# Products of zeros on TensorE around the transposes of norms and in the attention's last steps

## The chip, the cores and the metric

One core of one Trainium2 chip runs the whole program. The metric is the device time of one execution in microseconds (us); the median of the timed executions stands for a kernel.

## What is computed

A sequence of 256 tokens with 1024 features goes through one block of a first model and two layers of a second, all in float32:

```python
# first model, one block
h = rmsnorm(x, norm_mix);  proj = h @ w_in
x = x + concat([hgrn2(...), rglru(...), gla(...)]) @ w_out
h = rmsnorm(x, norm_ffn)
x = x + (gelu(causal_dwconv(h @ ffn_w_gate)) * (h @ ffn_w_val)) @ ffn_w_down
x = rmsnorm(x, norm_final)
# second model, two layers
x = layer_norm(alpha * x + 0.5 * swiglu(x, w_gu[0], w_down[0]))
mix = token_mixers(x)        # window, latent (MLA), axial and differential attention, then @ w_out
x = layer_norm(alpha * x + mix)
x = layer_norm(alpha * x + 0.5 * swiglu(x, w_gu[1], w_down[1]))
```

The hidden width of the first feed-forward block is 2688 (21 tiles of 128), of the four others 2816 (22 tiles).

## The kernel before

**Precision.** Every large product is made of three with operands rounded to a shorter float (`F32R`): high by high, high by low and low by high (`mm3`, L782 to L785; `gate_up` joins two of them, L849 and L852). ScalarE rounds a weight tile (`weights_high`, L1316; `down_weights_high`, L1323), VectorE subtracts to get the rest (L1665, L1670). TensorE is the engine that has most to do.

**Order.** Each engine runs one program written out by hand, and they meet through semaphores. TensorE takes its instructions strictly in the order of `tensor_program`: a wait holds everything behind it. There are eight PSUM banks of 128 x 512 float32.

**Norm and transpose.** A norm is worked out on VectorE token by token, in two halves of 128 tokens (m = 0, 1). `turn(src, event, m)` (L787 to L794) then transposes the normed half on TensorE, eight 128 x 128 blocks (L793), the first four when `normed_v` says that columns 0 to 511 are there. ScalarE copies the bank, rounded (`turned_high`, L1328), VectorE subtracts (`turned_low`, L1680), and only then may the products with the normed half begin (`wait_h`, which waits for `h_low`).

**Feed-forward blocks.** `ffn(f, i, src)` (L894): f = 0 is that of the first model and turns both halves before its first product. For f = 1 to 4 the first two tiles are made per half (`gate_up_tokens`): half 0 is turned, both tiles are made for it, half 1 is turned, both tiles are made for that. The other tiles follow with all 256 tokens (`gate_up`), each with the `down` products of the tile before. With f = 1 and 3 the norm ahead follows another feed-forward block, with f = 2 and 4 it follows the attention's output product.

**Attention.** `first_projections(l)` (L1062) turns half 0, makes a chunk of the input projection for it, turns half 1, and goes on. `mixers(l)` then works through 20 units of attention (four window, four axial, eight differential, four MLA: units 0 to 19), in steps s = 0 to 20 (L1259). In step s TensorE makes, in this order: for even s the logits of units s+2 and s+3 (`logits`, L1190); the weighted sum of values of unit s-1 (`weighted`, L1221), which waits for ScalarE's copy of the transposed probabilities (L1596); while there are any, other projections; and the transposes of unit s's probabilities (`probabilities`, L1201). Steps 9 to 12 also transpose MLA's queries and keys into bank 5 (`latent_turn`, L1146), from where VectorE copies them out (L2100, signal `qk_copied`; the last is `qk_copied[l, "mla", 1, 2]`, in step 12). The exponentials are ScalarE's (L1585), the maxima VectorE's (L2057). In steps 17, 18 and 19 parts of the output product follow the probabilities (`out_part`).

`zeros` is a tile of 128 x 512 in bf16, all zero, which GpSimd clears at the very start; it is used by one product in `outputs` (L984).

Of the kernel before, what the change touches and what calls it, by code (L numbers as in the profile page):

```python
# [14 lines left out]
P = 128  # L15
# [153 lines left out]
def program(nc, A, C, out):  # L169
    ctx = ExitStack()  # L170
    with ctx:
        def sb(name, shape, dt=F32):
            return ctx.enter_context(nc.sbuf_tensor(name, shape, dt))

        bank = [ctx.enter_context(nc.psum_tensor(f"bank{i}", [P, HALF], F32)) for i in range(8)]
        signals = []

        def signal(name):
            signals.append(Signal(ctx.enter_context(nc.semaphore(name))))
            return signals[-1]  # L180
# [57 lines left out]
        qk_turned, qk_copied = signal("qk_transposed"), signal("qk_copied")  # L238
# [33 lines left out]
        zeros = sb("zeros", [P, HALF], BF16)  # L272
# [148 lines left out]
        def high_of(c):  # L421
            return (hi_out2 if third_place(c) else hi_out3) if outside_ring(c) else hi_gu[c % 2]

        def low_of(c):
            return (lo_out2 if third_place(c) else lo_out3) if outside_ring(c) else lo_gu[c % 2]
# [9 lines left out]
        def cols_view(t_, c):  # L435
            return t_[:, :].rearrange("p (k n) -> p k n", k=KD)[:, :, 0:width_of(c)]

        def pair_view(t_, c):
            return t_[:, :].rearrange("p (w k n) -> p w k n", w=2, k=KD)
# [40 lines left out]
        def tile_no(f, j):  # L480
            return FFN_FIRST[f] + j
# [5 lines left out]
        def wait_low(eng, c):  # L487
            s = wt_low_p if c in low_by_pool else wt_low_v
            eng.wait_ge(s.sem, s[c])
# [35 lines left out]
        def turn_bank(event, m, q):  # L525

            if event in (1, 2) or (isinstance(event, int) and event % 3 != 0):
                f = {1: 0, 2: 1}.get(event, 2 * ((event - 3) // 3) + (2 if event % 3 == 1 else 3))
                g1 = (FFN_FIRST[f] + 1) % 2
                return bank[(4 + g1, 6 + g1)[q]] if m == 0 else bank[q]  # L530
            if not isinstance(event, int):
                return bank[(6, 4)[q] + m]
            return bank[4 + 2 * m + q]
# [246 lines left out]
        def tensor_program(pe):  # L780

            def mm3(o, lhs, rhs, start, stop, **kw):  # L782
                pe.matmul(o, lhs[0], rhs[0], start=start, stop=False, **kw)  # L783
                pe.matmul(o, lhs[0], rhs[1], start=False, stop=False, **kw)  # L784
                return pe.matmul(o, lhs[1], rhs[0], start=False, stop=stop, **kw)  # L785

            def turn(src, event, m):  # L787

                for q in range(2):
                    if isinstance(event, int):  # L790
                        pe.wait_ge(normed_v.sem, normed_v[event, m, q])
                    for k in range(4 * q, 4 * q + 4):
                        t = pe.transpose(turn_bank(event, m, q)[:, (k % 4) * P:(k % 4 + 1) * P], src[:, m, k * P:(k + 1) * P], ident[:, :])  # L793
                    t.then_inc(h_turned.sem, h_turned.one((event, m, q)))  # L794

            def wait_h(event, m, k):
                if k % 4 == 0:
                    pe.wait_ge(h_low.sem, h_low[event, m, k // 4])
# [25 lines left out]
            def token_half(c, m, o, event=None):  # L824
                hv, lv = cols_view(high_of(c), c), cols_view(low_of(c), c)
                ms_ = slice(m * P, (m + 1) * P)
                wait_low(pe, c)
                for k in range(KD):
                    if event is not None:
                        wait_h(event, m, k)  # L830
                    i = mm3(o, (xTh[:, k, ms_], xTl[:, k, ms_]), (hv[:, k, :], lv[:, k, :]), k == 0, k == KD - 1)
                i.then_inc(tok_done.sem, tok_done.one((c, m)))
# [22 lines left out]
            def turn_products(g):  # L855

                t = g % 2
                pe.wait_ge(prod_done.sem, prod_done[g])
                for m in range(M):
                    i = pe.transpose(bank[4 + t][:, S + m * P:S + (m + 1) * P], act32[:, t, m * P:(m + 1) * P], ident[:, :])  # L860
                i.then_inc(act_turned.sem, act_turned.one(g))

            def gate_up_tokens(f, j, m, event=None, turned=None):

                g, c = tile_no(f, j), CHUNK_NO["ffn", f, j]
                o = bank[(4, 6)[m] + g % 2][:, 0:S].rearrange("p (w n) -> p w n", w=2)
                hv, lv = pair_view(high_of(c), c), pair_view(low_of(c), c)
                ts = slice(m * P, (m + 1) * P)
                wait_low(pe, c)
                for k in range(KD):  # L870
                    if event is not None:
                        wait_h(event, m, k)
                    if turned is not None and k == KD // 2:
                        turn_products(turned)
                    i = mm3(o, (xTh[:, k, ts], xTl[:, k, ts]), (hv[:, :, k, :], lv[:, :, k, :]), k == 0, k == KD - 1)
                done = tok_gate_up if m == 0 else up_done
                i.then_inc(done.sem, done.one(g))
# [16 lines left out]
            def ffn(f, i, src):  # L894
                tail = range(FFN_TILES[f] - TAIL, FFN_TILES[f])
                turn(src, i, 0)
                if f == 0:
                    turn(src, i, 1)
                else:

                    gate_up_tokens(f, 0, 0, i)
                    gate_up_tokens(f, 1, 0)
                    turn(src, i, 1)
                    gate_up_tokens(f, 0, 1, i)
                    gate_up_tokens(f, 1, 1, turned=tile_no(f, 0))
                    down(f, 0, 0)
                    turn_products(tile_no(f, 1))
                    down(f, 0, 1)
                for j in range(BY_TOKENS if f else 0, FFN_TILES[f]):
                    gate_up(f, j, i if j == 0 else None)  # L910
                    if 0 < j <= tail[0]:
                        for m in range(M):
                            down(f, j - 1, m)
                for m in range(M):
                    for j in tail:
                        down(f, j, m)
# [146 lines left out]
            def first_projections(l):  # L1063

                i = 3 + 3 * l
                c = CHUNK_NO["in2", l, 0]
                turn(x, i, 0)
                token_half(c, 0, bank[0][:, 0:WCOLS], i)
                turn(x, i, 1)

                pe.wait_ge(x_added.sem, x_added[i, 1, 0])
                token_half(c + 1, 0, bank[2][:, 0:width_of(c + 1)])
                token_half(c, 1, bank[1][:, 0:WCOLS], i)
                token_half(c + 1, 1, bank[3][:, 0:width_of(c + 1)])

            def mixers(l):
# [182 lines left out]
                for s in range(units + 1):  # L1259
                    if s + 2 < units and s % 2 == 0:  # L1260
                        logits(s + 2)
                    if s >= 1:
                        weighted(s - 1)
                    if s < len(BESIDE):
                        half(*BESIDE[s])
                    if s < units:
                        probabilities(s)
                    if s in (0, 1):
                        axial_turn(s)
                    if s == 2:  # L1270
                        latent_sums()
                    if 3 <= s <= 6:
                        up_projection((s - 3) // 2, (s - 3) % 2)
                    if 9 <= s <= 12:
                        latent_turn((s - 9) // 2, 2 * ((s - 9) % 2))
                    if s in (10, 11):
                        turn_mix(s - 10, 0)
                    if s == units - 3:

                        pe.wait_ge(exp_ok.sem, exp_ok[l, units - 3])  # L1280
                        out_part(1, 0, 0)
                        out_part(1, 1, 0)
                    if s == units - 2:
                        pe.wait_ge(exp_ok.sem, exp_ok[l, units - 2])
                        out_part(0, 0, 0)
                        out_part(0, 1, 0)
                    if s == units - 1:
                        pe.wait_ge(exp_ok.sem, exp_ok[l, units - 1])
                        out_part(0, 2, 0)
                        out_part(0, 3, 0)  # L1290
# [949 lines left out]
```

## Time and profile before

| | |
|---|---|
| median of 3 timed runs | 1430.88 us (1430.53 to 1436.68) |
| device time of the profiled execution | 1435.12 us |
| its span, first to last instruction | 1433.5 us |
| TensorE matmul busy | 1351.0 us, 94% of the span |
| VectorE busy | 917.1 us, 64% |
| ScalarE busy | 725.6 us, 51% |
| mean granted TensorE clock | 0.968 of full speed |

All times within the execution count from the span's start. "Busy" of TensorE counts the modelled ends of pipelined matmuls, so one of 128 x 512 is shown as 393 ns long while the next one starts 230 ns after it; the distance of starts is what an instruction costs. The granted clock is 1.0 at 2.4 GHz and 0.5 at 1.2 GHz; no other value occurs in this trace.

### The profile page before, as it was taken

Reading aid. Unit: us, or ns where it says so; the run is one execution under the profiler, and the core shown is the slowest. Engines: PE = TensorE matmul, PEld = TensorE weight load, DVE = VectorE, ACT = ScalarE, POOL = GpSimd, SP = SyncE. Lnnn points to the kernel's source line nnn. Section 1 sums busy time; section 2 is a strip of 40 time slices with the busy share of each in tenths; the row PEclk is TensorE's granted clock in tenths of the full one; section 3 lists DMA queues with packets and bytes.
Section 4 is the critical chain, followed back from the end, with each engine's and each line's share of the span. In section 5 each row is a group of like instructions: output and inputs, shape, how many; then the busy total and the mean of one; then the engine's idle time right before and its main releaser. Section 6 shows DMA issues by size and latency. Waiting matters only on the chain.

```text
span 1433.5 us, 20478 instructions
## 1 busy us (share of the span) xinstructions
PE 1351.0 (94%) x8221; PEld 1193.1 (83%) x8222; DVE 917.1 (64%) x1342; ACT 725.6 (51%) x1142; POOL 93.7 (7%) x137
## 2 busy tenths in 40 slices
PE   6888899998899999999899999999999999899997
PEld 6777888886788888888888888888888888888886
DVE  4787776777656658555666567656667464666556
ACT  5566455554455553564354554555553653354452
POOL 1233000000000000510000000000001400000000
PEclk9997999999999999998999999999999997999999
DMA  7333476665575664432476665666654332375661
GB/s 231 94 113 103 123 214 208 206 185 172 152 219 177 183 188 113 142 118 63 120 235 182 198 204 151 181 203 202 182 162 128 97 118 64 113 235 177 197 200 44
DMA packets 301191, 229.17 MB, mean 160 GB/s; under 512 B 13083, under 2 KB 283818, under 8 KB 301098
## 3 DMA queue, kind: packets, MB, share of 16 engines
q1 hardware_dynamic: 301082, 227.88, 52.8%
q8 instruction: 65, 1.06, 0.3%
q14 instruction: 28, 0.23, 0.0%
q10 hardware_dynamic: 16, 0.00, 0.0%
HBM read 226.80 MB, written 1.05 MB: 159 GB/s over the span
## 4 chain that ended last, share of the span: by engine, by line
PE 70%; DVE 15%; ACT 9%; DMA 3%; issue 2%; POOL 1%; SPq 0%; DVEq 0%; ACTq 0%
PE bank L849 20%; PE bank L783 11%; PE bank L852 10%; PE bank L784 10%; PE bank L785 10%; DVE lo_gu L1665 5%; ACT hi_gu L1316 4%; PE bank L1221 3%; DMA st_dn<-in_ffn_w_down 2%; PE bank L1190 2%; DVE lo_dn L1670 2%; PE bank L1201 1%; DVE conv L1830 1%; DVE stats L1692 1%; DVE n L1715 1%
## 5 line engine op out<-in xcount | busy, mean ns | idle before, releaser
L849 PE MATMUL bank<-xT,hi_gu 128*128 128x512 f32 x1616 | 404.8, 393 | 4.9 <-DVE lo_gu L1665 4.3
L1665 DVE TENSOR_TENSOR lo_gu<-st_gu,hi_gu 128x2048 fp32r<-128x2048 f32 (+2 forms) x146 | 323.4, 2218 | 111.9 <-ACT hi_gu L1316 111.8
L849 PEld LDWEIGHTS bank<-xT,hi_gu 128*128 128x128 f32 x1616 | 297.0, 189 | 64.4 <-DVE lo_gu L1665 6.4
L1316 ACT ACTIVATE hi_gu<-st_gu 128x2048 fp32r<-128x2048 f32 (+3 forms) x147 | 270.2, 1843 | 0.5 <-DMA st_gu<-in_ffn_w_gu 0.3
L852 PEld LDWEIGHTS bank<-xT,lo_gu 128*128 128x128 f32 x1616 | 220.8, 191 | 15.9
L852 PE MATMUL bank<-xT,lo_gu 128*128 128x256 f32 x1616 | 225.5, 282 | 0.0
L783 PE MATMUL bank<-hi_dn,actTh 128*128 128x512 f32 x436 | 172.4, 395 | 9.2 <-DVE actTl L1842 4.7
L784 PE MATMUL bank<-lo_dn,actTh 128*128 128x512 f32 x436 | 170.8, 392 | 0.0
L785 PE MATMUL bank<-hi_dn,actTl 128*128 128x512 f32 x436 | 169.7, 389 | 0.0
L1833 DVE TENSOR_TENSOR act<-act,bank 128x256 f32<-128x256 f32 x101 | 42.6, 421 | 174.2 <-ACT act L1413 174.2
L1323 ACT ACTIVATE hi_dn<-st_dn 128x1024 fp32r<-128x1024 f32 x109 | 114.6, 1056 | 67.9 <-DMA st_dn<-in_ffn_w_down 67.9
L1670 DVE TENSOR_TENSOR lo_dn<-st_dn,hi_dn 128x1024 fp32r<-128x1024 f32 x109 | 132.7, 1221 | 17.3 <-ACT hi_dn L1323 16.8
L783 PE MATMUL bank<-hi_gu,xT 128*128 128x256 f32 (+1 forms) x416 | 126.2, 303 | 10.7 <-DVE xT L1680 9.4
L784 PE MATMUL bank<-lo_gu,xT 128*128 128x256 f32 (+1 forms) x416 | 123.1, 296 | 0.0
L785 PE MATMUL bank<-hi_gu,xT 128*128 128x256 f32 (+1 forms) x416 | 122.9, 295 | 0.0
L783 PEld LDWEIGHTS bank<-hi_dn,actTh 128*128 128x128 f32 x436 | 82.2, 188 | 25.8 <-DVE actTl L1842 6.3
L783 PEld LDWEIGHTS bank<-hi_gu,xT 128*128 128x128 f32 x416 | 85.9, 206 | 14.2 <-issue 9.8
L785 PEld LDWEIGHTS bank<-hi_dn,actTl 128*128 128x128 f32 x436 | 81.9, 188 | 17.9
L784 PEld LDWEIGHTS bank<-lo_dn,actTh 128*128 128x128 f32 x436 | 82.2, 189 | 13.3
L784 PEld LDWEIGHTS bank<-lo_gu,xT 128*128 128x128 f32 x416 | 85.8, 206 | 0.0
L785 PEld LDWEIGHTS bank<-hi_gu,xT 128*128 128x128 f32 x416 | 85.5, 206 | 0.0
L1403 ACT ACTIVATE nonlin<-bank 128x256 f32<-128x256 f32 x101 | 38.3, 379 | 92.7 <-PE bank L852 92.6
(270 smaller groups left out, 1823.7 us busy)
## 6 DMA issues: line engine op xcount, KB each, us to landing
st_gu<-in_ffn_w_gu SPq DMA_DIRECT2D x176, 512.0 KB, 5.2
st_dn<-in_ffn_w_down SPq DMA_DIRECT2D x109, 512.0 KB, 6.6
st_gu<-in_w_in SPq DMA_DIRECT2D x23, 1024.0 KB, 5.4
st_gu<-in_w_out SPq DMA_DIRECT2D x12, 1024.0 KB, 5.1
st_gu<-in_ffn_w_gate SPq DMA_DIRECT2D x21, 512.0 KB, 4.2
st_gu<-in_ffn_w_val SPq DMA_DIRECT2D x21, 512.0 KB, 5.5
st_gu<-in_w_in SPq DMA_DIRECT2D x10, 512.0 KB, 4.1
gb<-in_ln_g SPq DMA_DIRECT2D x6, 512.0 KB, 7.3
```

The source lines that it names most:

```text
L783: pe.matmul(o, lhs[0], rhs[0], start=start, stop=False, **kw)
L784: pe.matmul(o, lhs[0], rhs[1], start=False, stop=False, **kw)
L785: return pe.matmul(o, lhs[1], rhs[0], start=False, stop=stop, **kw)
L849: pe.matmul(b[:, :], hv[:, w, k, :], xT[:, k, :, :].rearrange("p a b -> p (a b)"), start=k == 0, stop=k == KD - 1, skip_group_check=True)
L852: i = pe.matmul(b[:, 0:S], lv[:, w, k, :], xTh[:, k, :], start=False, stop=k == KD - 1, skip_group_check=True)
L1221: t = pe.matmul(bank[4][:, z * HD:(z + 1) * HD], ptb[:, u % 2, (2 * z + kt) * P:(2 * z + kt + 1) * P], vb[:, kt, v0 + vh * HD:v0 + (vh + 1 ...
L1316: i = act.activation(high, staged, ACT.Copy)
L1323: act.activation(hi_dn[g % RING][:, :], st_dn[g % 2][:, :], ACT.Copy).then_inc(dn_high.sem, dn_high.one(g))
L1403: act.activation(nonlin[:, t, :], gate[:, S:2 * S], ACT.Copy).then_inc(gate_side.sem, gate_side.one(g))
L1665: i = dve.tensor_tensor(low, staged, high.bitcast(F32), ALU.subtract)
L1670: dve.tensor_tensor(lo_dn[g % RING][:, :], st_dn[g % 2][:, :], hi_dn[g % RING][:, :].bitcast(F32), ALU.subtract).then_inc(dn_low.sem, dn_l ...
L1833: dve.tensor_tensor(act32[:, t, :], act32[:, t, :], up[:, 0:S], ALU.add).then_inc(own_v.sem, own_v.one())
```

## The change

A helper `fill(b, count)` issues `count` products of the tile of zeros into a bank that nobody reads at that time. Each is 128 x 128 by 128 x 512 in bf16. No other instruction, wait, buffer or transfer is changed, but for one added wait: in step 13 of each attention, ahead of the first fill into bank 5, TensorE waits for VectorE's copy of the last MLA keys out of that bank.

```diff
+            def fill(b, count):
+                for _ in range(count):
+                    pe.matmul(bank[b][:, :], zeros[:, 0:P], zeros[:, :], start=True, stop=True, skip_group_check=True)
...
             def ffn(f, i, src):
                 tail = range(FFN_TILES[f] - TAIL, FFN_TILES[f])
                 turn(src, i, 0)
+                idle = 6 + tile_no(f, 0) % 2
+                fill(idle, 3)
                 if f == 0:
                     turn(src, i, 1)
+                    fill(idle, 4)
                 else:
                     gate_up_tokens(f, 0, 0, i)
                     gate_up_tokens(f, 1, 0)
+                    fill(idle, 4)
                     turn(src, i, 1)
+                    fill(idle, 3)
                     gate_up_tokens(f, 0, 1, i)
...
                 turn(x, i, 0)
+                fill(7, 3)
                 token_half(c, 0, bank[0][:, 0:WCOLS], i)
+                fill(7, 6)
                 turn(x, i, 1)
...
                 for s in range(units + 1):
                     if s + 2 < units and s % 2 == 0:
                         logits(s + 2)
+                    if s >= 13:
+                        if s == 13:
+                            pe.wait_ge(qk_copied.sem, qk_copied[l, "mla", 1, 2])
+                        fill(5, 2)
                     if s >= 1:
                         weighted(s - 1)
```

Products of zeros added: 7 in block f = 0, 10 in each of f = 1 to 4, 9 in each of the two `first_projections`, and 16 in the steps 13 to 20 of each attention: 97 in all.

## Rows read from the trace of the kernel before

**Rows 1.** The page: the chain that ended last, share of the span by engine.

```profile
PE 70%; DVE 15%; ACT 9%; DMA 3%; issue 2%; POOL 1%; SPq 0%; DVEq 0%; ACTq 0%
```

**Rows 2.** Windows: stretch, us, busy of PE, PEld, DVE, ACT, POOL (count), PEclk, DMA.

```profile
170.00:176.80 6.80, 5.93 (x18) 4.79 (x19) 6.64 (x9) 4.37 (x5) 0.00 (x0) 0.50 0.25 74
...
1183.70:1204.20 20.50, 19.13 (x74) 16.95 (x74) 9.21 (x23) 7.47 (x22) 0.00 (x0) 0.50 0.00 1
1241.70:1248.60 6.90, 6.06 (x29) 6.03 (x29) 4.39 (x7) 4.53 (x8) 0.00 (x0) 0.51 0.40 123
```

**Rows 3.** The same view: just ahead of one fall, and a stretch without one.

```profile
702.40:705.80 3.40, 1.75 (x12) 1.31 (x13) 2.69 (x4) 1.84 (x3) 0.00 (x0) 1.00 0.19 46
...
634.20:637.60 3.40, 2.53 (x24) 2.29 (x23) 2.54 (x5) 2.76 (x10) 0.00 (x0) 1.00 0.00 0
```

**Rows 4.** Timeline of TensorE, f = 2, 4, 1: start, us, line, tiles [idle before, releaser].

```profile
703.20 1.32 PE L793 MATMUL bank<-ident,x 128*128 128x128 f32 x8 [1.97 <-DVE x L1722]
714.15 0.50 PE L783 MATMUL bank<-hi_dn,actTh 128*128 128x512 f32 x1 [1.10 <-DVE actTl L1812]
...
1240.44 1.32 PE L793 MATMUL bank<-ident,x 128*128 128x128 f32 x8 [1.97 <-DVE x L1722]
1252.54 0.50 PE L783 MATMUL bank<-hi_dn,actTh 128*128 128x512 f32 x1 [1.10 <-DVE actTl L1812]
...
370.01 0.36 PE L783 MATMUL bank<-hi_gu,xT 128*128 128x256 f32 x1 [1.07 <-DVE xT L1680]
377.32 0.50 PE L783 MATMUL bank<-hi_dn,actTh 128*128 128x512 f32 x1 [1.10 <-DVE actTl L1812]
```

**Rows 5.** The same view, the first two turns of f = 1 and f = 3.

```profile
362.09 0.36 PE L783 MATMUL bank<-hi_gu,xT 128*128 128x256 f32 x1 [0.84 <-DVE xT L1680]
367.91 1.04 PE L793 MATMUL bank<-ident,x 128*128 128x128 f32 x8
...
890.22 0.55 PE L783 MATMUL bank<-hi_gu,xT 128*128 128x256 f32 x1 [0.84 <-DVE xT L1680]
897.54 1.03 PE L793 MATMUL bank<-ident,x 128*128 128x128 f32 x8
```

**Rows 6.** The same view, second turn ahead of each attention, and a later wait in it.

```profile
557.04 1.32 PE L793 MATMUL bank<-ident,x 128*128 128x128 f32 x8 [1.85 <-DVE x L1722]
591.54 1.10 PE L1221 MATMUL bank<-proj,big 128*128 128x64 f32 x8 [0.45 <-ACT big L1596]
...
1086.67 1.32 PE L793 MATMUL bank<-ident,x 128*128 128x128 f32 x8 [1.84 <-DVE x L1722]
1124.33 1.10 PE L1221 MATMUL bank<-proj,big 128*128 128x64 f32 x8 [0.45 <-ACT big L1596]
```

**Rows 7.** Timeline, layer 1: VectorE's copy of step 12, TensorE in steps 14 to 17.

```profile
1180.50 0.69 DVE L2100 TENSOR_SCALAR big<-bank 96x512 f32<-96x512 f32 x1
...
1183.47 3.49 PE L1190 MATMUL bank<-big 96*128 96x256 f32 x8 [1.21 <-ACT big L1585]
...
1192.72 3.62 PE L1190 MATMUL bank<-big 96*128 96x256 f32 x8
1196.13 1.81 PE L1221 MATMUL bank<-proj,big 128*128 128x64 f32 x8
...
1201.95 0.56 PE L783 MATMUL bank<-hi_gu,xT 128*128 128x256 f32 x1
```

**Rows 8.** Timeline of layer 0's steps 14 to 17, TensorE.

```profile
650.68 3.19 PE L1190 MATMUL bank<-big 96*128 96x256 f32 x8 [1.21 <-ACT big L1585]
...
662.28 1.00 PE L1221 MATMUL bank<-proj,big 128*128 128x64 f32 x8
664.42 1.10 PE L1221 MATMUL bank<-n,big 128*128 128x64 f32 x8 [0.69 <-ACT big L1596]
...
665.72 0.36 PE L783 MATMUL bank<-hi_gu,xT 128*128 128x256 f32 x1
```

**Rows 9.** Chain of waits: start, us, eight products of 128 x 512, rounded operands, full speed.

```profile
392.37 1.84 PE bank L849 x8
```

## The prediction, as it was put on record

> **What bounds the kernel now.** I read the page first: TensorE carries 70% of the chain that ended last [rows 1] and is busy for 94% of the span. VectorE and ScalarE come in where TensorE waits for a norm, for a copy of transposed probabilities, or for weights in block f = 0. So two things can shorten this kernel: less waiting of TensorE, or more work per microsecond while it runs. The second view is the granted clock by windows. Its mean is 0.968, and there are only two levels, 2.4 and 1.2 GHz. Cutting the trace where the level changes gives seven stretches at 1.2 GHz in places that the change touches: 170.0 to 176.8 (f = 0), 651.3 to 661.5 (layer 0's last steps), 705.9 to 709.3 (f = 2), 890.2 to 893.6 (f = 3), 1088.2 to 1095.0 (ahead of layer 1's attention), 1183.8 to 1204.2 (layer 1's last steps) and 1241.8 to 1248.6 (f = 4). The first, the longest and the last stand in [rows 2]. They add up to 58 us, nearly all with TensorE busy. Four more lie before 143 us, which the change leaves alone.
>
> The third view is what TensorE did just before a fall. Ahead of that at 705.9 it was busy for 1.75 of 3.40 us and half of that were transposes; in a stretch at 634.2 it was busy for 2.53 of 3.40 us with small products, and the clock stayed up [rows 3]. So falls follow stretches in which TensorE waits once or twice for one or two microseconds and does little between. The same places in the other layer or block are not always hit: f = 1 and the projections ahead of layer 0's attention kept 2.4 GHz. That gives a clean twin for most places, and I price the falls by these twins, not by the length of a stretch.
>
> **What the falls cost.** All are differences of start times between a slowed place and its twin at full speed.
> - f = 2: from the second turn to the first `down` product 714.15 - 703.20 = 10.95 us; f = 1 takes 377.32 - 367.91 = 9.41 [rows 4, 5]. Lost: 1.5 us.
> - f = 4: 1252.54 - 1240.44 = 12.10 us [rows 4]. Lost: 2.6 us (its turn begins as f = 2's does; 0.1 taken off for that turn's own wait between its quads, in both).
> - f = 3: from the first product to the second turn 897.54 - 890.22 = 7.32 us against 367.91 - 362.09 = 5.82 in f = 1 [rows 5]. Lost: 1.5 us.
> - Ahead of layer 1's attention: 1124.33 - 1086.67 = 37.66 us against 591.54 - 557.04 = 34.50 in layer 0 [rows 6]. Lost: 3.2 us. Nothing in between gives it back; this is measured past every copy on the other engines.
> - Last steps. At full speed one pair of steps (logits, then twice a weighted sum and a set of transposes) is 665.72 - 662.28 = 3.44 us for all but the logits [rows 8], with one wait of 0.69 inside, plus the logits, which take 1196.13 - 1192.72 = 3.41 at 1.2 GHz [rows 7], so an estimated 1.7 at 2.4. A pair: 5.15 us; the steps 14 to 17 are two pairs, 10.3 us. Layer 0 took 665.72 - 650.68 = 15.04 (lost: 4.7), layer 1 took 1201.95 - 1183.47 = 18.48 (lost: 8.2), and it stayed slow for another 2.3 us of dense output products, half of which is lost: 9.3 in all. I take 9.0, since a little of that ending shows as overlap.
> - f = 0: no twin. TensorE is busy for 5.93 us at 1.2 GHz [rows 2], so 3.0 us at most. But the chain through this block runs over VectorE, ScalarE and the `down` weights' transfers, not over TensorE; what moves this chain is only the turn, whose eight transposes take 1.32 us at full speed [rows 4], so about 0.7 us more at half. I take 0.7, the lower end, because the chain is what ends later waits there.
>
> Sum if every one of these falls is avoided: 0.7 + 4.7 + 1.5 + 1.5 + 3.2 + 9.0 + 2.6 = 23.2 us.
>
> **What the products of zeros cost.** No row times a bf16 product of zeros. The nearest is the rounded 128 x 512 product at full speed, eight in 1.84 us, 0.23 us each [rows 9]; bounds are 0.2 and, if it runs at 1.2 GHz, 0.46. I take 0.23. Each group is set against the wait it stands in.
> - Three after a turn, 0.7 us: the wait there is 0.84 or 1.07 us [rows 4, 5], ended by VectorE's subtraction, which does not start later for it. Hidden; at 1.2 GHz they would stick out by 0.5.
> - Four ahead of the second turn, 0.9 us: in f = 2 and 4 the wait is 1.97 us [rows 4]; hidden. In f = 1 and 3 there is no wait before the second turn [rows 5]: the norm was done in time. There the four stand bare, and ScalarE's and VectorE's work on the turned half starts as much later. 0.9 us each, 1.8 in all.
> - f = 0: three in a wait of over 2 us, four in the one after the second turn; hidden, the latter barely.
> - Ahead of the attentions: three in a wait like the 0.84 one, six (1.4 us) in the wait of 1.85 [rows 6]. Hidden.
> - Steps 13 to 20, two each. Step 13 adds a wait for VectorE's copy, which ends at 1181.19 [rows 7]; unit 12's weighted sum started at 1180.72, so it starts about a microsecond later, and behind it unit 13's transposes. But TensorE then waited 1.21 us for an exponential before the next logits [rows 7], and that exponential does not hang on the delayed steps. Cost: 0, up to 0.5. Steps 15 and 17 have the wait of 0.69 ahead of the weighted sum [rows 8]: two products are 0.46, hidden. Steps 14 and 16 put them behind the logits, which already hide the copy, and steps 18 to 20 behind dense output products: no wait, so bare. Five steps x 2 x 0.23 = 2.3 us per layer, 4.6 in all.
>
> Sum: 1.8 + 4.6 = 6.4 us. Queues of the other engines and all transfers keep their order; they are released earlier or at most 0.9 us later.
>
> **The sum.** Against the profiled execution's own 1435.12 us: 1435.1 - 23.2 + 6.4 = 1418.3. Two kinds of sparse stretch get no fill: the differential units at about 632 and 1165 us, and waits of block f = 0 near 338 and 351 us. In this trace no fall followed them, but their like did elsewhere. I add 1.7 us for one short fall: 1420. The profiled execution lies 4.2 us above the median of 1430.88; I don't shift for that, because which places are hit seems to vary by execution (three runs span 6 us), and with the fills in place there is less left to vary.
>
> **A rule that speaks against.** The falls here come after single waits of 1.0 to 2.6 us. The Trainium skill ("TensorE: Matmul & The Clock Gate", "Why this matters for your kernels") asks only that TensorE not idle for one gap longer than any of these. By that rule these waits cause no fall and filling them helps nothing; the trace disagrees, with seven falls in just these places. Its Part 1 also says that operands of all zeros don't trip another limiter, of current; whether zeros count as activity for this clock no row here shows.
>
> **The rivals.**
> 1. *The zeros don't hold the clock, and cost.* The falls stay, and the bare products are paid, those at 1.2 GHz doubly: 6.4 us, plus 0.5 to 1 us for steps 14 and 16 of both layers, plus 0.5 each in places where a covered group sticks out of its wait in a slowed turn: about 8. Place: the steps 14 to 20, where TensorE is the bound. 1435.1 + 8 = 1443, or 1439 against the median. It decides as soon as fewer than 6.4 us of falls are avoided. For it: no row shows zeros raising the clock. Against: even light products at 634.2 held it [rows 3].
> 2. *Norms are cured, the last steps are not.* Two products are only 0.46 us, and the wait ahead of step 14's logits keeps most of its length. Then 9.5 us are won around norms and 6.4 to 8 us paid: 1433.
> 3. *The gain is handed on.* The falls go, but ScalarE's exponentials or VectorE's weight splits become the bound in the last steps and in f = 0, and half of the steps' 13.7 us is lost again: 1427. Against: in layer 0 from 662.28 on the steps ran at full speed with only the 0.69 waits [rows 8].
>
> **Chances.** Forecast (1415 to 1424) 0.64; rival 1 0.10; rival 2 0.10; rival 3 and partial cures 0.16. The range 1413 to 1431 takes in the forecast with its bounds (f = 0 giving 3.0 instead of 0.7; fills at 0.2; two or three leftover falls) and rival 3; it leaves out 1 and 2. A measurement can tell about 0.5%, so faster means below 1423.7 and slower above 1438.0 us: faster 0.70, same 0.22, slower 0.08.
>
> **What would show it.** In the profile after, the seven stretches should stand at 1.0, with the distances above at 9.4 (f = 2 and 4, second turn to `down`), 34.5 (second turn to step 0's wait) and about 11.2 us for steps 14 to 17 (10.3 and two bare pairs). A turn at f = 1 and 3 0.9 us later than its twin shows the bare fours. If the level still falls behind filled waits, zeros don't count or are too few; if it stays up and the time doesn't move, look for a new wait on ScalarE at L1585 or L1596. The forecast is wrong if a fill costs well over 0.23 us, or if new falls appear in the unfilled stretches.

## The result and the profile after

The changed kernel takes 1419.38 us (median of 14 runs, 1417.01 to 1423.47) against 1430.7 us for the kernel before, measured beside it (14 runs, 1421.86 to 1440.82). The ratio is 0.9916, with a 95% interval from 0.989 to 0.994: faster by 0.8%. The forecast was 1420 us, and its range 1413 to 1431. What the medians don't say is how much steadier the time became: 19 us between the fastest and the slowest run before, 6.5 us after.

| | before | after |
|---|---|---|
| device time of the profiled execution | 1435.12 us | 1417.01 us |
| its span | 1433.5 us | 1415.4 us |
| TensorE matmul busy | 1351.0 us | 1350.2 us |
| mean granted TensorE clock | 0.968 | 0.986 |

TensorE is busy for the same time with 97 products more, because the other products have become shorter. The page of the changed kernel, chain by engine, where [rows 1] stood before:

```profile
PE 70%; DVE 16%; ACT 9%; issue 2%; DMA 2%; POOL 1%; SPq 0%; DVEq 0%; ACTq 0%
```

The shares of the chain have hardly moved. Nothing was taken off it by a shorter dependency; the same chain is walked faster.

Windows of the changed kernel (stretch, us, busy of PE, PEld, DVE, ACT, POOL with counts, PEclk, DMA share, GB/s): the steps 14 to 17 of both layers, the second turn of f = 2, and the two stretches around the second turn of f = 0.

```profile
649.80:661.10 11.30, 10.79 (x72) 8.88 (x73) 8.13 (x20) 5.78 (x20) 0.00 (x0) 1.00 0.01 2
1174.90:1186.20 11.30, 10.79 (x72) 8.88 (x73) 8.21 (x20) 5.78 (x20) 0.00 (x0) 1.00 0.01 2
701.00:704.40 3.40, 3.21 (x25) 2.61 (x23) 2.90 (x4) 3.32 (x5) 0.00 (x0) 1.00 0.03 5
...
166.50:169.90 3.40, 1.50 (x12) 0.87 (x10) 2.89 (x8) 1.29 (x3) 0.00 (x0) 1.00 0.00 0
170.00:173.30 3.30, 3.30 (x12) 2.05 (x11) 3.25 (x6) 2.47 (x4) 0.00 (x0) 0.50 0.00 0
```

Layer 1's steps, which had 0.50 for 20.5 us [rows 2], are at 1.00. Of the seven slowed stretches six are gone. The one at the start of f = 0 is left, half as long as before, and in this execution a fall of 3.4 us at 337 us is new. Apart from these two only the falls before 143 us remain, which the change doesn't touch, and one from 1412.4 us to the end, where TensorE has no work left (the kernel before had it too, from 1429.5 us).

The timeline of the changed kernel's TensorE at the places of [rows 4 to 8] (start, us, line, tiles, idle before and its releaser; the line of every added product is L799):

```profile
891.25 1.04 PE L799 MATMUL bank<-zeros 128*128 128x512 bf16 x4
892.12 1.04 PE L793 MATMUL bank<-ident,x 128*128 128x128 f32 x8
892.99 0.81 PE L799 MATMUL bank<-zeros 128*128 128x512 bf16 x3
894.22 0.36 PE L783 MATMUL bank<-hi_gu,xT 128*128 128x256 f32 x1 [0.42 <-DVE xT L1699]
...
697.79 1.04 PE L799 MATMUL bank<-zeros 128*128 128x512 bf16 x4
699.92 1.32 PE L793 MATMUL bank<-ident,x 128*128 128x128 f32 x8 [1.09 <-DVE x L1741]
709.37 0.50 PE L783 MATMUL bank<-hi_dn,actTh 128*128 128x512 f32 x1 [1.10 <-DVE actTl L1831]
...
1225.02 1.32 PE L793 MATMUL bank<-ident,x 128*128 128x128 f32 x8 [1.09 <-DVE x L1741]
1234.46 0.50 PE L783 MATMUL bank<-hi_dn,actTh 128*128 128x512 f32 x1 [1.10 <-DVE actTl L1831]
...
1081.22 1.32 PE L793 MATMUL bank<-ident,x 128*128 128x128 f32 x8 [0.53 <-DVE x L1741]
1115.72 1.10 PE L1235 MATMUL bank<-proj,big 128*128 128x64 f32 x8 [0.45 <-ACT big L1615]
...
1172.63 0.61 PE L799 MATMUL bank<-zeros 128*128 128x512 bf16 x2 [0.78 <-DVE big L2119]
1174.86 1.96 PE L1204 MATMUL bank<-big 96*128 96x256 f32 x8 [0.34 <-ACT big L1604]
1176.66 0.60 PE L799 MATMUL bank<-zeros 128*128 128x512 bf16 x2
1178.38 0.59 PE L799 MATMUL bank<-zeros 128*128 128x512 bf16 x2
1179.22 1.11 PE L1235 MATMUL bank<-proj,big 128*128 128x64 f32 x8 [0.26 <-ACT big L1615]
1182.34 0.60 PE L799 MATMUL bank<-zeros 128*128 128x512 bf16 x2
1182.78 1.00 PE L1235 MATMUL bank<-proj,big 128*128 128x64 f32 x8
1186.21 0.36 PE L783 MATMUL bank<-hi_gu,xT 128*128 128x256 f32 x1
```

Two kinds of added product can be told apart here. The four at 697.79 end before the wait for the norm does: the idle time ahead of the turn went from 1.97 [rows 4] to 1.09 us, and the turn didn't move. The four at 891.25 have no idle time behind them: the turn starts 0.87 us later, four times 0.218 us, and everything after it too. In the steps, the pair at 1178.38 only shortens a wait (0.69 to 0.26), the pair at 1182.34 is followed at once by the weighted sum, which starts 0.44 us after it.

**Where the time went**, as differences of the two profiles between starts of the same instruction (before minus after; gains positive):

| stretch | forecast | measured |
|---|---|---|
| up to f = 0's second turn (untouched) | 0 | 0.6 |
| f = 0, to its end | 0.7 | 1.2 |
| f = 1 (bare four) | -0.9 | -0.9 |
| ahead of layer 0's attention and its steps to 13 | 0 | 0 |
| layer 0, steps 14 to 17 | 4.7 - 0.9 | 3.7 |
| layer 0, steps 18 to 20, to f = 2's second turn | -1.4 | -1.3 |
| f = 2's second turn to first `down` | 1.5 | 1.5 |
| f = 3, net of its bare four | 0.6 | 0.6 |
| ahead of layer 1's attention | 3.2 | 3.2 |
| layer 1, steps 14 to 20, to f = 4's second turn | 9.0 - 2.3 | 6.8 |
| f = 4's second turn to first `down` | 2.6 | 2.7 |
| sum | 16.8 | 18.1 |

These are two single executions. The one before took 4.4 us more than the median of its kernel, the one after is the fastest of its 14; so they differ by 18.1 us and the medians by 11.3.

The new fall at 337 us cost nothing. TensorE at that place, first in the kernel before, then in the changed kernel:

```profile
338.74 2.12 PE L849 MATMUL bank<-xT,hi_gu 128*128 128x512 f32 x8 [2.48 <-DVE lo_gu L1665]
351.95 0.50 PE L783 MATMUL bank<-hi_dn,actTh 128*128 128x512 f32 x1 [2.90 <-DVE actTl L1842]
...
336.98 3.62 PE L854 MATMUL bank<-xT,hi_gu 128*128 128x512 f32 x8 [2.15 <-DVE lo_gu L1684]
350.19 0.51 PE L783 MATMUL bank<-hi_dn,actTh 128*128 128x512 f32 x1 [1.68 <-DVE actTl L1861]
```

Eight products took 3.62 instead of 2.12 us, but the changed kernel is 1.76 us ahead at the first pair of lines and 1.76 us ahead at the second: the wait at 350 us became shorter by what the fall took.

### The profile page after: what moved, and what is told of

Read it like the earlier page. It is cut to its first block, busy times and chain, and to the rows that moved or that the text cites. A ratio compares the mean times of both kernels' runs of the same rounds, so it can differ in the third digit from the quotient of the medians.

```text
span 1415.4 us, 20673 instructions
## 1 busy us (share of the span) xinstructions
PE 1350.2 (95%) x8319; PEld 1182.6 (84%) x8319; DVE 917.4 (65%) x1342; ACT 724.6 (51%) x1142; POOL 92.8 (7%) x137
## 4 chain that ended last, share of the span: by engine, by line
PE 70%; DVE 16%; ACT 9%; issue 2%; DMA 2%; POOL 1%; SPq 0%; DVEq 0%; ACTq 0%
PE bank L854 20%; PE bank L857 11%; PE bank L783 10%; PE bank L784 10%; PE bank L785 10%; DVE lo_gu L1684 5%; ACT hi_gu L1335 4%; PE bank L1235 2%; DVE lo_dn L1689 2%; PE bank L1204 2%; DMA st_dn<-in_ffn_w_down 2%; DVE conv L1849 1%; PE bank L1215 1%; DVE stats L1711 1%; DVE n L1734 1%
## 5 line engine op out<-in xcount | busy, mean ns | idle before, releaser
L783 PE MATMUL bank<-hi_gu,xT 128*128 128x256 f32 (+1 forms) x416 | 121.6, 292 | 4.2 <-DVE xT L1699 2.9
L784 PE MATMUL bank<-lo_gu,xT 128*128 128x256 f32 (+1 forms) x416 | 118.9, 286 | 0.0
L785 PE MATMUL bank<-hi_gu,xT 128*128 128x256 f32 (+1 forms) x416 | 118.6, 285 | 0.0
L783 PEld LDWEIGHTS bank<-hi_gu,xT 128*128 128x128 f32 x416 | 81.1, 195 | 10.3 <-issue 6.6
L1432 ACT ACTIVATE act<-bank 128x256 f32<-128x256 f32 x101 | 38.2, 378 | 88.9 <-PE bank L857 88.9
L783 PE MATMUL bank<-xT,hi_gu 128*128 128x256 f32 x248 | 73.4, 296 | 8.3 <-ACT proj L1502 4.5
```

Of the source, the lines that this page charges most:

```text
L1432: act.activation(act32[:, t, :], up[:, S:2 * S], ACT.Copy).then_inc(up_side.sem, up_side.one(g))
```

## The experiments

Each kernel was timed beside the kernel before on the same chip, in four sets of runs: one for `e1` to `e4`, one for `e5` to `e8`, one for `e9` to `e11`, one for `e12`. The medians of the kernel before in them were 1430.6, 1435.9, 1431.1 and 1430.2 us. `C` stands below for the changed kernel.

**Norms alone, steps alone.** `e1_norms` leaves out the products of the steps:

```diff
-                    if s >= 13:
-                        if s == 13:
-                            pe.wait_ge(qk_copied.sem, qk_copied[l, "mla", 1, 2])
-                        fill(5, 2)
```

> The products of zeros around the norms' transposes stay (65), those in steps 13 to 20 and their wait are gone (32 fewer). My theory (each group only hinders falls of the clock at its own place): no half-clock stretch at the starts of f = 1 to 4 and ahead of the attentions; the last steps of the attentions fall in some executions, up to 4.7 us in layer 0 and 9 us in layer 1, while 4.6 us of bare products are saved. So about 1421 us with a wide spread (1413 to 1428). Rival (the fills of the steps did most of the work): 1427 or more.

Measured: 1417.45 us median of 11 runs, 1415.24 to 1430.08. `e2_steps` leaves out every `fill` around a `turn`:

```diff
                 turn(src, i, 0)
-                idle = 6 + tile_no(f, 0) % 2
-                fill(idle, 3)
...
-                fill(7, 3)
                 token_half(c, 0, bank[0][:, 0:WCOLS], i)
-                fill(7, 6)
```

> Only the products of zeros in steps 13 to 20 stay (32); those around norms are gone. My theory: steps 14 to 17 keep 2.4 GHz in both layers, 11.5 us for both pairs; the starts of f = 2 and 4 and the second turn ahead of the attentions fall in most executions, of 9.5 us together about two thirds; 1.8 us of bare products in f = 1 and 3 saved: about 1424 us. Rival (norms alone matter, the steps' products only cost): 1435.

Measured: 1427.21 us median of 12 runs, 1419.07 to 1431.92. It lies 3 us above the 1424 that I expected and 8 below the rival's 1435. Windows of `e1_norms` (layer 0's last steps, then from f = 2's second turn, 704.11, on), and of `e2_steps` (f = 2's second turn, ahead of layer 1's attention, and layer 0's last steps):

```profile
652.20:662.20 10.00, 9.31 (x35) 8.11 (x34) 4.65 (x10) 3.51 (x14) 0.00 (x0) 0.50 0.00 1
704.10:711.00 6.90, 6.69 (x50) 5.86 (x51) 5.02 (x8) 4.99 (x8) 0.00 (x0) 1.00 0.24 75
```

```profile
706.30:713.00 6.70, 5.88 (x28) 5.80 (x28) 4.22 (x6) 4.55 (x8) 0.00 (x0) 0.50 0.37 112
1088.60:1098.70 10.10, 10.10 (x49) 9.96 (x48) 5.51 (x9) 1.19 (x2) 0.00 (x0) 0.50 0.39 104
650.00:661.00 11.00, 9.62 (x68) 8.04 (x69) 8.61 (x22) 6.35 (x17) 0.00 (x0) 1.00 0.00 1
```

Each group acts where it stands. Where the steps have none, layer 0's still ran for 10 us at 0.50; where the norms have none, both places after a second turn did, and the steps did not. The median of `e1_norms` is below `C`'s 1419.38, better than I expected: without the steps' 20 bare products 4.4 us are saved in every run, and the falls come back in some only. The slowest run, 1430.08 us, had a mean clock of 0.974, the fastest, 1415.24, one of 0.984; which places fell in the slowest can't be seen, since it has no trace. Against `e3_covered` below, which has twelve products in the steps but not the eight bare ones of f = 1 and 3 (1.7 us), the median, with these 1.7 us taken off, is only 2.3 us higher, the slowest run 13. So the steps' products save little in a typical execution and much in a bad one.

**Only the products that stand in a wait.** `e3_covered`:

```diff
-                    fill(idle, 4)
+                    if f % 2 == 0:
+                        fill(idle, 4)
...
-                        fill(5, 2)
+                        if s in (13, 15, 17):
+                            fill(5, 2)
```

> The changed kernel without the products that stand in no wait: the four ahead of the second turn in f = 1 and 3, and those of steps 14, 16, 18, 19 and 20. 69 products stay, all in waits. My theory: these 28 bare ones cost 28 x 0.22 = 6.2 us and hindered no fall, so 1413 us, with the clock at 1.0 in the same places. Rival (the bare ones in the steps keep the clock up, since the steps' waits are spread over all of them): falls come back in steps 14 to 17, 1418 us or more with a wider spread.

Measured: 1413.4 us median of 6 runs, 1411.16 to 1414.89; ratio to the kernel before 0.988 (0.985 to 0.992). Its windows over the last steps of layer 0 and the start of f = 2:

```profile
651.80:662.20 10.40, 9.89 (x67) 8.46 (x68) 8.01 (x20) 5.80 (x20) 0.00 (x0) 1.00 0.01 2
701.00:705.00 4.00, 3.80 (x30) 3.23 (x28) 3.69 (x4) 3.91 (x6) 0.00 (x0) 1.00 0.10 13
```

So 28 of the 97 products cost 6.0 us (1419.4 - 1413.4) and did nothing. The traces agree: from the first turn of f = 1 to the second of f = 4, `C` takes 1225.02 - 358.17 = 866.85 us and `e3_covered` 1221.80 - 361.09 = 860.71, which is 6.14 us less, 0.219 for each of the 28. The last steps' clock doesn't need them.

**Is it busy time, or any instruction?** `e4_thin` keeps the count and the places and cuts the length to 16 columns; `e6_half` cuts it to 256:

```diff
-                    pe.matmul(bank[b][:, :], zeros[:, 0:P], zeros[:, :], ...)
+                    pe.matmul(bank[b][:, 0:16], zeros[:, 0:P], zeros[:, 0:16], ...)    # e4_thin
+                    pe.matmul(bank[b][:, 0:S], zeros[:, 0:P], zeros[:, 0:S], ...)      # e6_half
```

> The same 97 products of zeros in the same places, each with 16 columns in place of 512: the same count, the same weight loads, hardly any busy time. If what holds the clock is how long TensorE is kept busy (my theory), the falls stay as in the kernel before: about 1431 us, plus at most 28 x 0.06 = 1.7 us for bare ones, with the wide spread of the kernel before. If it is enough that TensorE is given some instruction in a wait (rival), the falls go: about 1413 us.

Measured: 1429.19 us median of 12 runs, 1420.72 to 1438.04; ratio to the kernel before 0.999 (0.996 to 1.002). The line of the added products in its trace (duration in ns, least, median and most; first and last start), and its windows over layer 1's last steps and the start of f = 2:

```profile
L799 PE MATMUL bank<-zeros x97: 169/170/221, 168.8 to 1241.1; 128*128 128x16 bf16 x97
1182.40:1202.70 20.30, 19.01 (x81) 17.07 (x79) 8.85 (x22) 6.95 (x21) 0.00 (x0) 0.50 0.00 1
701.00:707.80 6.80, 6.30 (x32) 5.96 (x31) 4.48 (x7) 4.81 (x7) 0.00 (x0) 0.50 0.20 65
```

All 97 are there and the falls are too. It is not the instruction but how long it occupies the array.

> The same 97 products in the same places with 256 columns in place of 512: half the busy time. If it is the busy time that holds the clock, halving it makes part of the falls come back (mostly at the starts of f = 2 and 4 and at step 14, hardly ahead of the attentions, where nine products stand), while the bare ones cost 28 x 0.11 = 3 us less: about 1420 us with a wide spread, 1414 to 1428. If full length was more than needed: 1416 us with the narrow spread of the changed kernel.

Measured: 1416.96 us median of 9 runs, 1415.36 to 1420.15, with a spread as narrow as `C`'s. The expectation of falls coming back was mostly too gloomy: its trace has none at the starts of f = 1 to 4. One came where only two products stand, at 1173.6 us in the logits of layer 1's step 14, and was over at 1177.0, at that step's pair (1176.53); f = 0's, which full length doesn't cure either, is there too. The 2.4 us below `C` are most of what the bare ones cost less (28 x 0.11 = 3.1). Full length was more than the norms' waits needed.

**The price of a bare product.** `e5_price` adds a hundred where TensorE has no wait:

```diff
                 wait_low(pe, c)
+                if f in (1, 3) and 5 <= j < 10:
+                    for _ in range(10):
+                        pe.matmul(gate[:, :], zeros[:, 0:P], zeros[:, :], start=True, stop=True, skip_group_check=True)
```

> The changed kernel with 100 more products of zeros in dense stretches: ten each ahead of the gate products of tiles 5 to 9 of f = 1 and f = 3, where TensorE is the bound and has no wait, so each costs its full price. If a bare product costs 0.22 us, as the distances in the changed kernel's trace say, 1419.4 + 22 = 1441 us; if it costs 0.23 or more, 1442.5 or more; if VectorE's and ScalarE's work had slack to hide it, less.

Measured: 1442.44 us median of 12 runs, 1438.08 to 1444.59. Two of its tiles on the timeline:

```profile
426.73 2.33 PE L850 MATMUL bank<-zeros 128*128 128x512 bf16 x10
428.71 2.18 PE L857 MATMUL bank<-xT,hi_gu 128*128 128x512 f32 x8
431.68 2.00 PE L857 MATMUL bank<-xT,hi_gu 128*128 128x512 f32 x8
437.22 2.33 PE L850 MATMUL bank<-zeros 128*128 128x512 bf16 x10
```

A tile takes 437.22 - 426.73 = 10.49 us, against 8.31 without (400.68 - 392.37 in the chain of the kernel before): 0.218 us each, so 21.8 for a hundred. The medians say 23.1 (1442.44 - 1419.38), but the two kernels were timed in different sets of runs. Nothing hides them.

**Where the fall in the steps is fought.** `e8_no13` takes from `e3_covered` step 13's two products and the added wait; `e9_only13` takes those of steps 15 and 17:

```diff
-                    if s >= 13:
-                        if s == 13:
-                            pe.wait_ge(qk_copied.sem, qk_copied[l, "mla", 1, 2])
-                        if s in (13, 15, 17):
-                            fill(5, 2)
+                    if s in (15, 17):          # e8_no13
+                        fill(5, 2)
...
-                        if s in (13, 15, 17):
+                        if s == 13:            # e9_only13
                             fill(5, 2)
```

> The kernel with the covered products alone, without those of step 13 and the wait added there; steps 15 and 17 keep theirs. If the sparse stretch of steps 13 and 14 is what starts the fall (my theory), it is now as bare as in the kernel before: the fall comes in some executions, but steps 15 and 17 are busier than before, so it may end sooner: median 1415 us, highest above 1420. If the products of steps 15 and 17 carry the effect, or the fall has no fixed origin: 1413 us with the narrow spread.

Measured: 1412.53 us median of 6 runs, 1411.62 to 1413.56. The narrow spread is what the rival said, and no fall in the steps stands in its trace. Theory B of the next expectation was formed on this.

> The kernel with the covered products alone, without those of steps 15 and 17: of the last steps only step 13 has its two products and its wait. Theory A (they hinder the fall where it starts, between steps 13 and 14): about 1413 us with the narrow spread of the covered kernel. Theory B, after the kernel without those of step 13 stayed at 1412.5 us within 2 us, and the changed kernel's repeat e5 showed one fall at 647 us that ended after 3.4 us: the products of steps 15 and 17 don't stop the fall, they end it early. Then without them a fall here lasts as long as in the kernel before, 10 to 20 us in some executions: median 1414 to 1418 us, the highest above 1420.

Measured: 1413.9 us median of 6 runs, 1413.2 to 1415.66: theory B's long falls didn't come. One of its premises was a misreading as well: the fall at 647.3 us in the trace of `e5_price` is not one of the last steps. The added products delay that kernel, so that its step 13 begins with the pair at 660.64 us; the fall lies among the differential units, where no product of zeros stands, and ended without one. By `e8_no13` and `e9_only13` alone either group seems to be enough. The next kernels say more.

**More of it.** `e7_more` adds to `e3_covered`:

```diff
-                fill(idle, 3)
+                fill(idle, 7 if f == 0 else 3)
...
+                if f == 0 and j == 19:                       # gate_up
+                    pe.wait_ge(gate_summed.sem, gate_summed[g - 2])
+                    fill(4 + g % 2, 6)
                 wait_low(pe, c)
...
+                        if f == 0 and m == 0 and j == tail[-1]:
+                            fill(5, 7)
                         down(f, j, m)
...
+                if lev == 0:                                 # levels of the first model's scores
+                    pe.wait_ge(cleared_p.sem, cleared_p["zeros"])
+                if lev in (3, 6, 8):
+                    copied = t_copied_a if lev == 3 else tok_copied_a
+                    pe.wait_ge(copied.sem, copied[{3: 7, 6: 10, 8: 11}[lev], 0])
+                    fill(6, 6)
...
+            pe.wait_ge(selected.sem, selected[LEV_N - 1, 0, 0])
+            fill(0, 5)
             pe.wait_ge(selected.sem, selected[LEV_N - 1, 3])
...
+                    if s == 9:
+                        wait_projected(pe, l, 8, 0)
+                        fill(6, 3)
```

> The kernel with the covered products alone (1413.4 us), and more of them in waits that had none: ahead of levels 3, 6 and 8 of the first model's scores and of the last head outputs, seven instead of three between the two turns of f = 0, six and seven in the two waits at the end of f = 0, and three ahead of the weighted sum of step 9. In the trace of the covered kernel 20 us at half clock remain in those places before 145 us and at 352 us, of which some 15 us are within reach. My theory: most of them go and half their length is won, 1408 us. Rival (they collide with the copies that the added waits ask for, or VectorE and ScalarE bind there and nothing is won): 1413 to 1416 us.

Measured: 1410.72 us median of 6 runs, 1410.12 to 1412.56; ratio 0.986 (0.981 to 0.991). The fastest version of the study, but the gain over `e3_covered` is 2.7 us where I expected 5. Windows of its repeat (`e12_more_again`, below):

```profile
50.00:57.00 7.00, 3.67 (x17) 3.67 (x18) 3.96 (x4) 3.99 (x6) 2.60 (x1) 0.65 0.00 0
112.00:119.00 7.00, 6.59 (x64) 5.44 (x66) 6.63 (x10) 1.66 (x4) 0.73 (x1) 1.00 0.42 138
130.00:142.00 12.00, 9.13 (x65) 8.16 (x65) 8.23 (x15) 7.11 (x9) 5.83 (x3) 0.86 0.39 132
```

The kernel before and `e3_covered` went through the place at 112 us at half clock. That it is cured is not shown by this window: the trace of `C` has 1.00 there too, without a product, and fell at 81.2 us instead. But each of the eleven traces without these additions has a short fall somewhere between 80 and 121 us, and none of the three with them. The place at 50 us follows a wait of 4.5 us into which I found no bank to put a product; at 134.1 us a fall is left, and another follows at 147.7.

What was gained can be placed by the traces. Block f = 0, from its second turn to the first turn of f = 1, takes 187.7 to 187.8 us in the three traces with the additions, 189.6 in that of `e3_covered` and 188.3 to 190.0 in all with three products between its turns. What lies before it gained 0.1 us in `e7_more` and 1.4 in `e12_more_again`, against `e3_covered`.

`e10_best` is the same without step 13's products and wait:

> The kernel with more products in more waits, without those of step 13 and its wait. If each part does what it did alone (1410.7 us for more, 0.9 us less without step 13): 1410 us, between 1409 and 1412. If step 13's products are needed after all: a spread beyond 4 us.

Measured: 1414.36 us median of 6 runs, 1410.71 to 1416.19. Its profiled execution shows why. Timeline of TensorE from step 13 on, and one window:

```profile
647.27 0.61 PE L1229 MATMUL bank<-ident,big 128*128 128x128 f32 x4
649.08 3.71 PE L1218 MATMUL bank<-big 96*128 96x256 f32 x8 [1.21 <-ACT big L1618]
652.59 1.80 PE L1249 MATMUL bank<-proj,big 128*128 128x64 f32 x8
655.04 1.05 PE L799 MATMUL bank<-zeros 128*128 128x512 bf16 x2
655.93 1.10 PE L1249 MATMUL bank<-proj,big 128*128 128x64 f32 x8
657.32 1.89 PE L1218 MATMUL bank<-big 96*128 96x256 f32 x8
649.20:655.90 6.70, 6.70 (x22) 5.18 (x22) 4.50 (x8) 1.80 (x7) 0.00 (x0) 0.50 0.00 0
```

The wait of 1.21 us ahead of step 14's logits is whole again, the fall comes right after it, and it is over at the next pair of products, in step 15, after 6.7 us instead of 10 to 20. It cost 2.9 us: step 14's logits start 0.48 us later than in the trace of `e12_more_again` (649.08 against 648.60), the first turn of f = 2 starts 3.40 us later (689.90 against 686.50). The repeat of `e7_more` was to tell chance from cause:

> The kernel with more products in more waits, step 13's included, once more and on another start. If the products of step 13 are what keeps the fall away there (theory A), it stays within 3 us of spread around 1411 us, as in its first job, where the same kernel without them spread over 5.5 us. If that spread was chance, it is now as wide as that one, with a median near 1413 us.

Measured: 1410.93 us median of 6 runs, 1410.26 to 1412.21, at a ratio of 0.986 (0.982 to 0.991). Twelve runs with step 13's products now span 2.4 us, six without them 5.5 us, and four of these six are slower than all twelve. I read it so: step 13's two products hinder the fall, and those of step 15, when it has come, are followed by its end. Neither half is shown. For the first, `e8_no13` against `e3_covered` says the opposite (1.9 us of spread without them, 3.7 with them), and that its six runs just didn't meet the fall is my guess. For the second there are two falls, this one and that of `e6_half`; and in the kernel before layer 0's fall ended at 661.5 us, in the middle of the steps, with no product of zeros near.

Last, the changed kernel again, on the chip of `e9_only13` and `e10_best`:

> The changed kernel once more, on the chip of the two others. Against it the bare products' price is read without a change of chip: 1419.4 us within 1.5, so 6 us above the kernel with the covered ones alone, and its trace shows which falls are left in an execution with another start.

Measured: 1419.19 us median of 12 runs, 1416.51 to 1423.03; 5.3 us above `e9_only13` beside it, which leaves out the same 28 bare products and four covered pairs. Its trace, of an execution of 1420.46 us, has two short falls between 145 us and the end of TensorE's work: at the start of f = 0 (172.0 to 175.4 us) and at 352.9 us, late in the same block. It is 1.94 us behind the first trace of `C` at the second turn of f = 0 (171.55 against 169.61), 3.34 at the second turn of f = 1 (370.37 against 367.03) and 3.36 at that of f = 4 (1228.38 against 1225.02). So these two executions of the changed kernel differ by what happened before f = 1; behind it they keep the same distance to 0.1 us.

## Why the prediction was right

The likeliest case held, and so did its terms for f = 1 to 4 and for both attentions. That for f = 0 and the allowance did not. The slip in the third view (transposes are 1.32 of the 1.75 busy us ahead of f = 2's fall, three quarters and not half) bears on no term.

- *Falls are the cost, priced by twins.* Right, to 0.1 us in f = 2, f = 4 and ahead of the attention: 709.37 - 699.92 = 9.45 and 1234.46 - 1225.02 = 9.44 us against the twin's 9.41, and 1115.72 - 1081.22 = 34.50 against 34.50. Two half-clock stretches of unequal length (3.4 us in f = 2, 6.8 in f = 4) were worth 1.5 and 2.7 us; the twins gave that without a guess on how much of a stretch TensorE was the bound.
- *A pair of steps at full speed.* Predicted 11.2 us for steps 14 to 17 with two bare pairs, measured 1186.21 - 1174.86 = 11.35. The logits took 1176.66 - 1174.86 = 1.80 us where I had halved 3.41 to 1.7.
- *f = 0.* 0.7 forecast, 1.2 measured, but not as it was forecast: the fall was halved, not avoided, so this stretch was the one of seven that didn't stand at 1.0. Three products between the turns leave 1.90 us idle there, and a fall followed, also in the second trace of `C`. At half clock the four behind the second turn stuck out: from that turn to the first gate product it took 172.54 - 169.61 = 2.93 us, 2.62 before (172.84 - 170.22). From its second turn on the block takes 188.6 us in one trace of `C`, 190.0 in the other and 189.7 before, so the difference between 1.2 and 0.7 is within its scatter.
- *What the products cost.* 0.23 taken, 0.218 by the trace; 28 bare ones at 6.4 us forecast, 6.0 by the median of `e3_covered`, 6.1 by its trace.
- *The added wait.* Step 13's weighted sum starts late, at 1173.08, and step 14's logits wait 0.34 instead of 1.21 us: nothing lost, as said.
- *The allowance of 1.7 us for a fall elsewhere.* The places were right: `C` fell at 337 us in one trace and at 352.9 in the other, and `e5_price` among the differential units. The price was not: the fall at 337 cost nothing, since a wait behind it took it in. That 1420 is nearer to the median of 1419.4 than the sum without the allowance, 1418.3, is luck.
- *The starting point.* The falls of one slow execution (1435.1 us) were priced, and nothing was shifted to the median of 1430.7. That held because little of what varied was left once they were gone. It doesn't make 23 us the typical loss: with 6.1 us paid for bare products and 11.3 won, the medians say some 17, and in the steps, priced at 13.7, `e1_norms` says that a typical execution loses far less.

**The rivals.** That zeros don't hold the clock is excluded: only the length of the same products separates `C` (1419.4) from `e4_thin` (1429.2). "Norms cured, steps not" is `e1_norms` in its slower runs, but not `C`. "Handed on" didn't happen; ScalarE's copies end inside waits that are now 0.26 us. That short waits are harmless, as the Trainium skill's rule was read ("TensorE: Matmul & The Clock Gate", "Why this matters for your kernels"), doesn't hold here: `e4_thin` has the same waits and the same instructions with 16 columns, and the falls come.

**What I left out** is the size of the chance in the kernel before. Its time is a draw: over the 76 runs beside the experiments it took from 1419.4 to 1441.0 us, and the mean granted clock of a run tells the time. Runs at 0.964 took 1437.6 to 1441.0, runs at 0.977 and above 1419.4 to 1424.9; a straight line gives 13 us for each 0.01 of clock, correlation -0.93. The best of them are as fast as the median of `C`: they met few falls, and had no bare products to pay. Without these the change is better than luck: all six runs of `e3_covered` (1411.2 to 1414.9) are faster than the fastest of the 76.

## What to carry to other kernels

Where TensorE is the bound, read the granted clock by stretches and compare a slowed place with its twin at full speed: the difference of start times is the gain to be had, whatever the length of the slowed stretch. A wait of 1 to 2 us with little around it can be filled with products into an idle bank, as many as end before the wait does: these are free, and they took 17 to 20 us off here (1430.7 to 1413.4 with 69 products, to 1411 with 115), while each one outside a wait cost its full 0.22 us and brought nothing. And when runs of one kernel spread by over 1%, look at the clock of each before comparing medians.

## What the runs showed of the hardware

- Products of zeros hold the clock. The mean granted clock of a run was 0.964 to 0.979 in the 76 runs of the kernel before, 0.982 to 0.988 in the 14 of `C`, and 0.967 to 0.980 in the 12 with 16 columns in place of 512.
- A slowed stretch can outlast high busy time. With 16-column products layer 1's last steps stayed at 0.50 for 20.3 us, with TensorE busy for 19.0 of them, in products of 96 rows or 64 columns and transposes. Dense products of 128 rows and 256 columns followed, and then the clock rose. They are not needed for it: in the kernel before layer 0's fall ended after 10.2 us within the steps. In `e10_best` it rose after two products of 512 columns.
- A bf16 product of 128 x 512 among float32 ones costs 0.218 us, with its weight load (98 ns) hidden behind the product before it.
- How long a fall lasts makes most of its price where TensorE is the bound: 1.5 us for those that ended after 3.4 us in dense work, 8 to 9 us for layer 1's steps, at half clock for 20.5 us. Ahead of a wait that can take it in, a fall costs nothing: that at 337 us.
